# Two attention stages with transposes two units behind the scores, and new orders of work at the ends of three stages

## What is computed

```python
def swa_sink_attention(q, k, v, sinks):         # banded: 8 heads of 64, window 128
    ...
    sc = jnp.einsum('bnqkgd,bnjkd->bnkgqj', qb, kb).astype(jnp.float32) * (d ** -0.5)
    mask = (kpos <= qpos) & (qpos - kpos < w) & (kpos >= 0)
    sc = jnp.where(mask[None, :, None, None], sc, NEG_INF)
    p = jax.nn.softmax(jnp.concatenate([sc, sink], axis=-1), axis=-1)[..., :-1].astype(v.dtype)
    o = jnp.einsum('bnkgqj,bnjkd->bnqkgd', p, vb)

def forgetting_attention(q, k, v, fcum):        # 8 heads of 64, causal
    ...
        s = s + jnp.transpose(fq, (0, 2, 1))[..., None] - f_key[:, :, None, :]
        p = jax.nn.softmax(s, axis=-1).astype(v.dtype)

def even_mixer(h, ...):                         # before the latent attention:
    q = (rmsnorm(z_cq, q_norm) @ w_uq).reshape(b, s, MLA_HEADS, MLA_NOPE + MLA_ROPE)

def hgrn2_mixer(h, w_in, lb, gn_g, w_out):      # 8 heads, forward and backward scan
    ...
    o = o * lax.rsqrt(jnp.mean(o * o, axis=-1, keepdims=True) + EPS)
    o = o * gn_g.astype(jnp.float32).reshape(HGRN_HEADS, HGRN_DV)
    o = o.reshape(b_sz, s_len, D_MODEL).astype(h.dtype) * jax.nn.silu(g)
    return o @ w_out
```

## Time and profile before

| what | value |
|---|---|
| median of 3 runs | 2163.84 us (2163.27 to 2165.21) |
| the profiled execution | 2165.33 us, its span from the first to the last instruction 2163.5 us |
| PE busy | 2067.0 us, 96% of the span |
| DVE, ACT busy | 1459.0 us, 922.2 us |
| mean granted TensorE clock | 0.985 |

### The profile page before, as it was taken

One profiled execution on the slowest core, in us unless ns is written; L12 is line 12 of the kernel. 1 busy time (PEld: TensorE's weight loads), 2 busy tenths in 40 slices (PEclk: granted clock), 3 DMA queues, 4 the chain that ended last, 5 costly groups with the idle time before them and its releaser, 6 DMA issues.

```text
span 2163.5 us, 26466 instructions
## 1 busy us (share of the span) xinstructions
PE 2067.0 (96%) x9808; PEld 1589.4 (73%) x9808; DVE 1459.0 (67%) x2639; ACT 922.2 (43%) x1739; POOL 16.1 (1%) x15
## 2 busy tenths in 40 slices
PE   4989999999999999899999999999999899999998
PEld 2766566777667676578888887788888777888886
DVE  7667777666475799876555566989889865343343
ACT  3344554354443532343223235666666544232231
POOL 1000000000000000000000000000000000000000
PEclk8999999999999999999999999999999999999999
DMA  8522222533224111045555552111111122233221
GB/s 337 195 93 78 76 79 69 175 127 136 79 84 165 45 49 49 20 146 204 178 196 173 183 175 69 59 50 57 52 49 59 40 69 79 97 98 97 97 90 58
DMA packets 65982, 228.73 MB, mean 106 GB/s; under 512 B 7104, under 2 KB 9280, under 8 KB 65728
## 3 DMA queue, kind: packets, MB, share of 16 engines
q1 hardware_dynamic: 65856, 227.05, 30.9%
HBM read 224.93 MB, written 2.10 MB: 105 GB/s over the span
## 4 chain that ended last, share of the span: by engine, by line
PE 72%; DVE 17%; ACT 5%; issue 4%; DMA 1%; SPq 1%; DVEq 0%; ACTq 0%
PE bank L379 20%; PE bank L381 19%; PE bank L380 19%; DVE arena L1793 6%; PE bank L2079 3%; DVE w_lo L315 1%; PE bank L1242 1%; PE bank L688 1%; PE bank L1256 1%; PE bank L1267 1%; PE bank L987 1%; DMA arena<-ada_dram 1%; DVE arena L2025 1%; ACT w_hi L306 1%; ACT arena L1285 1%
## 5 line engine op out<-in xcount | busy, mean ns | idle before, releaser
L379 PE MATMUL bank<-h_hi,w_hi 128*128 128x512 f32 (+1 forms) x1564 | 643.1, 411 | 3.9 <-DVE h_lo L680 1.5
L381 PE MATMUL bank<-h_hi,w_lo 128*128 128x512 f32 (+1 forms) x1564 | 616.3, 394 | 0.0
L380 PE MATMUL bank<-h_lo,w_hi 128*128 128x512 f32 (+1 forms) x1564 | 614.5, 393 | 0.0
L306 ACT ACTIVATE w_hi<-w_raw 128x1024 fp32r<-128x1024 f32 (+3 forms) x293 | 290.7, 994 | 286.6 <-PE bank L381 273.6
L315 DVE TENSOR_TENSOR w_lo<-w_raw,w_hi 128x1024 fp32r<-128x1024 f32 (+3 forms) x290 | 333.3, 1151 | 73.9 <-ACT w_hi L306 73.5
L379 PEld LDWEIGHTS bank<-h_hi,w_hi 128*128 128x128 f32 (+1 forms) x1564 | 296.8, 190 | 71.9 <-issue 8.4
L381 PEld LDWEIGHTS bank<-h_hi,w_lo 128*128 128x128 f32 (+1 forms) x1564 | 295.6, 189 | 65.9
L380 PEld LDWEIGHTS bank<-h_lo,w_hi 128*128 128x128 f32 (+1 forms) x1564 | 296.8, 190 | 58.8 <-issue 3.8
L379 PE MATMUL bank<-a_hi_t,w_hi 128*128 128x512 f32 x512 | 203.0, 396 | 0.0
L380 PE MATMUL bank<-a_lo_t,w_hi 128*128 128x512 f32 x512 | 203.0, 396 | 0.0
L381 PE MATMUL bank<-a_hi_t,w_lo 128*128 128x512 f32 x512 | 203.0, 396 | 0.0
(11 more groups left out here) (276 smaller groups left out, 2496.2 us busy)
## 6 DMA issues: line engine op xcount, KB each, us to landing
w_raw<-weights_dram SPq DMA_DIRECT2D x261, 512.0 KB, 3.6
ada_raw<-ada_dram SPq DMA_DIRECT2D x128, 512.0 KB, 3.6
arena<-ada_dram SPq DMA_DIRECT2D x8, 1024.0 KB, 15.7
w_raw<-weights_dram SPq DMA_DIRECT2D x16, 256.0 KB, 2.5
xT<-x_dram SPq DMA_DIRECT2D x1, 2048.0 KB, 14.4
out_dram<-xT SPq DMA_DIRECT2D x8, 256.0 KB, 2.2
tables<-tables_dram SPq DMA_DIRECT2D x1, 1536.0 KB, 19.8
w_raw<-weights_dram SPq DMA_DIRECT2D x8, 144.0 KB, 3.5
```

The costliest lines, as they stand in the source:

```text
L306: nc.scalar.activation(WH[:, slot, 0:w], RAW[:, raw, 0:w], ACT.Copy).then_inc(w_hi_ready, 1)
L379: nc.tensor.matmul(o, WH[:, slot, cols], self.hi(k), start=(i == 0), stop=False)
L380: nc.tensor.matmul(o, WH[:, slot, cols], self.lo(k), start=False, stop=False)
L381: last = nc.tensor.matmul(o, WL[:, slot, cols], self.hi(k), start=False, stop=(i == self.K - 1))
```

## The change

1. `PairAttention` gets a parameter `lag`, 1 as before, and 2 in the banded and the forgetting attention. Transposes and PT copies of unit u-lag and sums of unit u-lag-1 stand with the scores of unit u. There are 2*lag+2 row buffers and columns of statistics, and the stage has two steps more.
2. In the banded attention's weave, `nq` writes its high part in place and its low part to free places, no longer over `HH` and `HL`. Its steps go from 26.7 to 14.7 and on, two apart; `pq` starts at 26.4 with 1.2 a tile, `nk` at 28.2.
3. In the forgetting attention's weave, the scratch of `hn` moves, and the seven blocks of `yp` go from 31.2 + 0.7i to 32.4 + 0.8i.
4. In head 7 of HGRN each slot splits one head's output, at the start of ACT's slot and not at its end; the blocks follow one slot later; a third tile's blocks go into the second direction's slots, and `HgrnEnd` gets a fourth tile's. The weight of the fourth tile is split ahead, in slots (1, 1) and (1, 2). Bank 6 serves as the fourth tile's bank. The norm behind it moves with it.

```diff
-                self.steps = 2 * U + 4
+                self.steps = 2 * U + 2 * lag + 2
...
-                if s % 2 == 0 and 2 <= u < U + 2:
-                    self.pe_sums(pe, u - 2)
-                if 1 <= u < U + 1:
-                    self.pe_turn(pe, u - 1, s % 2)
+                lag = self.lag
+                if s % 2 == 0 and lag + 1 <= u < U + lag + 1:
+                    self.pe_sums(pe, u - lag - 1)
+                if lag <= u < U + lag:
+                    self.pe_turn(pe, u - lag, s % 2)
...
-                if 1 <= u < U + 1:
-                    self.act_copy(act, u - 1, s % 2)
+                if self.lag <= u < U + self.lag:
+                    self.act_copy(act, u - self.lag, s % 2)
...
-                    if r >= 4:
-                        dve.wait_ge(self.turned.sem, self.turned.at(r - 3))
-                        dve.wait_ge(self.exp_ready.sem, self.exp_ready.at(r - 3))
+                    if r >= self.rows:
+                        dve.wait_ge(self.turned.sem, self.turned.at(r - self.rows + 1))
+                        dve.wait_ge(self.exp_ready.sem, self.exp_ready.at(r - self.rows + 1))
...
-            nq = Norm(Z[:, 0:3, :], 3, lambda k: vec("q_norm", k), None, HH, HL, 0, scratch=(view(16, (2, S)), view(20, (2, S)), None, view(28, (S,)), None),
+            NQ_HI = place_at("nq_hi", arena_offset + 48 * 1024, [P, 3, S], F32R)
+            NQ_LO = [place_at(f"nq_lo{k}", arena_offset + kb * 1024, [P, S], F32R) for k, kb in enumerate((44, 46, 76))]
+            nq_hi, nq_lo = lambda k: NQ_HI[:, k, :], lambda k: NQ_LO[k][:]
+            nq = Norm(Z[:, 0:3, :], 3, lambda k: vec("q_norm", k), None, nq_hi, nq_lo, 0, scratch=(view(16, (2, S)), view(20, (2, S)), None, view(28, (S,)), None),
...
-            weave((swa, 0, 1), (gates, 0.3, 0.8), (nq, 26.7, 0.3, 4, 8), (pq, 28.1, 0.9), (nk, 29.2, 1, 3, 6))
+            weave((swa, 0, 1), (gates, 0.3, 0.8), (nq, 14.7, 2, 4, 8), (pq, 26.4, 1.2), (nk, 28.2, 1, 3, 6))
...
-                  *((Do(lambda pe, i=i: yp.chunk(pe, i, range(3))), 31.2 + 0.7 * i, 1) for i in range(C - 1)))
+                  *((Do(lambda pe, i=i: yp.chunk(pe, i, range(3))), 32.4 + 0.8 * i, 1) for i in range(C - 1)))
...
-                    pr = Begun(8, C, P, HH, HL, [], residual(96 + 16), evac_engine="dve", chunks=H.split, outer=3)
-                    out = {"project": pr, (0, 1): ((0, 1), ()), (0, 2): ((2,), (0, 1)), (0, 3): ((3,), (2,)), (0, 4): ((4,), (3,)), (0, 5): ((5,), (4,)),
-                           (0, 6): ((), (5,)), (1, 0): ((6,), ()), (1, 1): ((), (6,))}
+                    pr = Begun(8, C, P, HH, HL, [], residual(96 + 16), evac_engine="dve", chunks=H.split, outer=4, banks=(0, 1, 2, 6), split_early=True)
+                    pr.before[3] = (H.applied.sem, H.applied.at(13))
+                    out = {"project": pr, (0, 1): ((0,), (), ()), (0, 2): ((1,), (0,), ()), (0, 3): ((2,), (1,), ()), (0, 4): ((3,), (2,), ()), (0, 5): ((4,), (3,), ()),
+                           (0, 6): ((5,), (4,), ()), (1, 0): ((6,), (5,), ()), (1, 1): ((), (6,), ()), (1, 2): ((), (), (0,)), (1, 3): ((), (), (1, 2)),
+                           (1, 4): ((), (), (3,)), (1, 5): ((), (), (4, 5)), (1, 6): ((), (), (6,))}
```

More of the change, by code:

```diff
@@ L443, in evacuate, with splits @@
                 self.evac(eng, bank[self.banks[t]], t, t % RING, t // 2, self.free)
+            def splits(self, t):
+                return t < self.count and self.n0 + t + AHEAD < N_TILES
             def act_step(self, act, i):
@@ L450, in act_tile @@
             def act_tile(self, act, t, p):
-                if t < self.count and p == 0 and self.n0 + t + AHEAD < N_TILES:
+                if self.splits(t) and p == 0:
                     split_hi(act, self.n0 + t + AHEAD)
@@ L467, in dve_tile @@
                     self.evacuate(dve, t)
-                if t < self.count and p == min(1, self.parts - 1) and self.n0 + t + AHEAD < N_TILES:
+                if self.splits(t) and p == min(1, self.parts - 1):
                     split_lo(dve, self.n0 + t + AHEAD)
@@ L499, in build, with __init__, early_hi, early_lo @@
         class Begun(Project):
+            def __init__(self, *args, split_early=False, **more):
+                Project.__init__(self, *args, **more)
+                self.split_early = split_early
+            def early_hi(self, act):
+                split_hi(act, self.n0 + AHEAD)
+            def early_lo(self, dve):
+                split_lo(dve, self.n0 + AHEAD)
+            def splits(self, t):
+                return Project.splits(self, t) and not (t == 0 and self.split_early)
             def chunk(self, pe, k, tiles=(0, 1)):
@@ L1187, in build, with __init__ @@
         class PairAttention(Stage):
-            def __init__(self, heads, scale, finish, e, pt, ready=(), window=False, sink=None, forget=None, made=None):
+            def __init__(self, heads, scale, finish, e, pt, ready=(), window=False, sink=None, forget=None, made=None, lag=1):
                 self.heads, self.scale, self.finish, self.E, self.PT = heads, scale, finish, e, pt
-                self.ready, self.window, self.sink, self.forget = ready, window, sink, forget
+                self.ready, self.window, self.sink, self.forget, self.lag, self.rows = ready, window, sink, forget, lag, 2 * lag + 2
                 self.made = made or {}
@@ L1210, in keys, with column @@
                 return range(i - 1 if self.window and i else 0, i + 1) if self.window else range(i + 1)
+            def column(self, which, r):
+                at = (8, 14, 20, 28)[which] + r % self.rows
+                return STAT[:, at:at + 1]
             def row_read(self, h):
@@ L1255, in pe_turn @@
                 for a in range(n):
-                    last = nc.tensor.transpose(bank[6][:, a * P:(a + 1) * P], self.E[r % 4][:, a * P:(a + 1) * P], ident)
+                    last = nc.tensor.transpose(bank[6][:, a * P:(a + 1) * P], self.E[r % self.rows][:, a * P:(a + 1) * P], ident)
                 last.then_inc(self.turned.sem, 1)
@@ L1307, in dve_step @@
                     return
-                done = u >= 2 and self.units[u - 2][1] == NT - 1
+                v = u - self.lag - 1
+                done = v >= 0 and self.units[v][1] == NT - 1
                 if done:
-                    g = self.units[u - 2][0]
-                    dve.wait_ge(self.out_done.sem, self.out_done.at(u - 1))
+                    g = self.units[v][0]
+                    dve.wait_ge(self.out_done.sem, self.out_done.at(v + 1))
                     self.finish.take(dve, g, self.out_read)
@@ L2223, in act @@
                 h, d = u // 2, u % 2
+                for k in self.out.get((d, l), ((), (), ()))[0]:
+                    H.high_act(act, k)
                 if l == 0:
@@ L2266, in act @@
                         H.key_act(act, u + 2)
-                for k in self.out.get((d, l), ((), ()))[0]:
-                    H.high_act(act, k)
+                    if not woven and l == 1:
+                        self.out["project"].early_hi(act)
             def dve(self, dve):
@@ L2321, in dve @@
                         H.times_sigmoid(dve, h, "g")
-                for k in self.out.get((d, l), ((), ()))[0]:
+                    if not woven and l == 2:
+                        self.out["project"].early_lo(dve)
+                for k in self.out.get((d, l), ((), (), ()))[0]:
                     H.low_dve(dve, k)
```

44 lines of the change are left out of this document (24 added, 20 removed).

## The result

The changed kernel takes 2170.29 us (median of 7 runs, 2168.32 to 2170.98) against 2163.84 in the same runs of the kernel before: ratio 1.0025, interval 1.0016 to 1.0035. It is slower by 0.25% where 0.5% faster was forecast. Its profiled execution had 2168.32 us, span 2166.5.

| stage, from which PE instruction to which | before | after | difference | forecast |
|---|---|---|---|---|
| banded: first score to the first score of the latent attention | 117.3 | 117.9 | +0.6 | -6.0 |
| forgetting: first score to the first sum of the norm behind `yp` | 151.2 | 158.9 | +7.7 | 0 |
| HGRN: last `pv_own` but one to the first sum of the norm behind `pr` | 80.3 | 74.8 | -5.4 | -4.9 |

The account below looks back on a forecast made before the run. PE was taken as the bound, busy 2067.0 of 2163.5 us, so only its idle or half-clock time could go. Banded -6.0, lag 0 and HGRN -4.9 sum to -10.9 us, from 2163.84 to 2153 (2149 to 2157), chance 0.50.

Parts of the forecast that it names:

- The lag in the forgetting attention: Forgetting attention: time saved at the first transpose is waited at the second, so 0 us, bounds -1.5 and +1.5.
- The banded stage: Banded attention: filling the idle hole at its end, less three costs, gives -6.0 us, bounds -8.1 and 0.
- I take all 8.1 us as removed: Banded attention's end: `pq` tiles cover 4.23 us of PE idle time and remove 3.9 lost at half clock.
- `nq` among the gate tiles: Banded attention, units 7 to 10: extra DVE scales and low parts delay maxima, +1.0 us, bounds 0 and 4.3.
- the last copy without cover: Banded attention's new end: last transpose, copy and sums have no tile between, so PE waits +0.6 us.
- the late `finish`: Banded attention's end: `finish` comes later against the next stage's rotary steps, +0.5 us, bounds 0 to 2.
- L1256 waits for L1297 outside that hole as before: Check for the banded attention: away from the filled hole, PE's transposes wait for ACT's copies as before.
- Lag in the banded stage: Banded attention: transposing two units behind the scores was to save nothing, 0 us.
- HGRN: HGRN's last head: earlier high parts and moved blocks fill PE's idle time, -4.9 us, bounds -10.6 and 0.
- C: Rival: the lag pays, removing remaining copy and weight waits and a half-clock stretch, -8.7 us, 2144; chance 0.14.
- D: Rival: the hole moves with `nq` and `pq`, the clock still falls, HGRN gives 1.5; 2162, no difference; chance 0.12.
- E: Rival: maxima come late at each of four `nq` places and the clock falls, +7 us, 2171; chance 0.06.

Follow-up runs that it names:

- x3: Changed kernel with only the banded attention back to lag 1, the forgetting one still at lag 2: 2168.95 us, ratio 1.0017 to the kernel before.
- x1: Changed kernel with both attentions back to lag 1 and the `yp` blocks at their old places: 2159.04 us, ratio 0.9975 to the kernel before.
- x2: Changed kernel with only the forgetting attention back to lag 1 and the old `yp` places: 2159.03 us, ratio 0.9978 to the kernel before.
- w2: Changed kernel, lag 2 kept, with the split behind the next unit's maxima and the last four `hn` parts later: 2160.52 us, ratio 0.9981.
- w1: Changed kernel with forgetting attention at lag 1, old `yp` places, and its split one unit later, where lag 2 puts it: 2162.55 us, ratio 0.9992.
- x4: Kernel before with only the new end of HGRN's last head: 2158.50 us, ratio 0.9967 to the kernel before.
- y4: Changed kernel with `nq`, `pq`, `nk` at old places, lag 2 in the banded attention and lag 1 in the forgetting one: 2163.64 us, ratio 0.9992.
- z4: Changed kernel with lag 1 in both attentions, old `yp` places, and the split behind the next unit's maxima: 2158.07 us, ratio 0.9977.
- z2: Changed kernel with lag 1 and old `yp` places in the forgetting attention, and the split behind the next unit's maxima: 2160.74 us, ratio 0.9973.
- y3: Changed kernel with forgetting attention at lag 1 and the modulation sums of `pq` behind its odd tiles: 2160.28 us, ratio 0.9977.

## Why the prediction was wrong

**The lag in the forgetting attention** (forecast 0, bounds -1.5 and +1.5; measured +7.7 in the stage, in the medians 9.9, `x3` against `x1`, to 11.3, after against `x2`). The step that failed is "I take 0 for the banded attention and 0 for the forgetting one", and in it the sum over one instruction pair. It followed transposes and copies, which the lag moves and which behave as said, and left out what else is tied to the older unit: the read of bank 7 and the split, 1.79 us of DVE, which moved a unit later and so ahead of the widest maximum. PE's queue, ACT's and DVE's were each walked for the transpose, DVE's not for `finish`. `finish` was named once, as a cost of 0.5 us at the stage's end. The runs showed in its place: +3.3 us idle and 11.1 us more at half clock (5.6 lost), less 1.1 that this sum does not explain (the idle time inside the slow stretches, 0.7 us, is counted one and a half times in it, which is 0.4). With the split moved behind the maxima the stage is 4.1 us shorter, with `hn` moved too 8.2 and as long as before; over both stages the two are worth 9.8 us of the changed kernel's time (`w2`). The split's place with lag 1 costs 1.4 us of idle time, and 3 to 3.5 us in time at the limit of what the runs can tell (`w1`). How much of the rest is the read of bank 7, which stands in front of PE's sums at once and can't be put off without delaying them, was not tried apart.

**The banded stage** (forecast -6.0, measured +0.6 in the profiles and nothing in the medians). "I take all 8.1 us as removed" is the step that failed. The hole and its slow stretch did go, and the clock gave more than forecast: 21.8 us at half level became 7.5, worth 7.2. But the idle time grew by 5.7 us. The largest waits are 2.97 for the read of bank 7 behind a weight's low part and a modulation tile, 2.52 for the maximum behind the split and `nk`, and 1.93 at 188.09 behind the split. Both figures lean on one execution of the kernel before: `x4`, with the same order of work there, had 11.4 us at half level and 13.2 idle. Nor is it the lag alone. `x1`, with the new order and lag 1, has 13.2 us idle too and a stage no shorter than `x4` (117.4 against 115.7): the 2.8 and the wait for `nq` are gone, and 1.3, 1.3 and 0.9 us stand at 209 to 213 in their place. Cover only helps if it stands ahead of the waiting instruction; the `pq` tiles stand between steps. The sizes for `nq` among the gate tiles (+1.0; 0.68 more idle, by `y4`), for the last copy without cover (+0.6; the sums waited 0.74 there) and for the late `finish` (+0.5; the rotary wait grew by 0.4) were of the right order. The check that I had named, "L1256 waits for L1297 outside that hole as before", came out wrong: 3.5 us (5.4 in `x4`) became 10.2.

**Lag in the banded stage** (forecast 0): 5 us with the old order of `nq` and `pq` (`y4` against `x4`), nothing with the new one (`x2` against `x1`).

**HGRN** (forecast -4.9, measured -5.4 in the trace, 5.8 in the medians of `x4`'s turns). The mechanism held: the waits for L2044 fell from 9.4 to 4.5 us, the one of 3.9 stayed at 3.8, and the fifth tile waits 0.39 us for its weight, where +0.4 was forecast and nothing stood before. The clock has no part in it: the stage has 3.4 us at half level in both kernels, and 11.6 us of idle time became 6.4. One sign came out otherwise: DVE still waits 1.96 us for the high part once (1728.87, against 4.13 before and the 1 us that the forecast asked for), at the cost of 0.38 us of PE. In all fifteen kernels with the new end this stage takes 74.1 to 74.9 us.

**Rivals.** C (the lag pays) did not occur: no pair of kernels that differ in the lag of one stage shows a gain in the medians. D came nearest for the banded stage: the hole moved. E had the right sum (2171) for the wrong reason: `nq` among the gate tiles added 0.68 us of waiting (`after` against `y4`) and there is no half-clock stretch between 165 and 185; the late maxima that cost most were two of the forgetting stage (627.79 and 656.24), behind the split. That ACT works its queue in order, which spoke against the lag, holds in the traces after ([6.78 <-DVE] and then the copies behind the exponential).

No version beats the simplest one by a margin that the runs can tell: `x4`, the kernel before with the HGRN end, at 2158.50 and 0.9967, is the simplest; the lowest median, 2158.07 and 0.9977, is `z4`'s. The parts in the two attentions can be left out.

## What to carry to other kernels

When a step is moved in hand-ordered queues, list everything that hangs on it, the work at the end of a group above all, and look at what it now stands in front of; 1.8 us ahead of the widest unit's maximum cost more than the 1.3 us wait that the move was to remove. Put work that nobody waits for behind the instruction on which the other engines wait: that one edit gave back 8.4 us of the changed kernel, though nothing that shows in the kernels with lag 1, where the work stood elsewhere. Before filling a hole, find the instruction that ends it, and ask whether the filler stands ahead of it in the waiting engine's queue.

## What the runs showed of the chip

The length of the forgetting stage is 141.7 us plus PE's idle time plus half of the time at half clock, in all kernels with lag 1 within 0.4 us, and 0.2 to 1.2 less with lag 2. Idle time inside the slow stretches explains at most 0.5 of that (0.7 us of it in the changed kernel, 0.9 in `x3`, 0.1 or none in the others); the rest stays open. The two terms make up the difference between 148.5 us (`x2`) and 158.9 to about 1.3 us. The Trainium skill ("TensorE: Matmul & The Clock Gate", section "Terms") prices the throttled time in just this way; as a sum over a stage with idle time beside it the traces agree with it to about 1 us.

A slow stretch can also hide waiting. `before` and `x4` have the same order of work in the banded stage and 21.8 against 11.4 us at half level, which would be 5.2 us of time; but they have 10.6 against 13.2 us idle, and the stages differ by 1.6. Within a slow stretch of `before` the transpose at 161.39 us waited 0.36 us, at full clock in `x4` the same one 1.61.

What I had not expected is how loosely the slow stretches go with the idle time. `x2` and `z2` have the same 4.8 and 4.9 us idle in the forgetting stage and 3.3 against 12.6 us at half clock. The executions of one kernel differ in the same way: of the eleven of `z2` five lie at 2154.2 to 2156.3 us and six at 2160.7 to 2162.3, and none between. Two slow stretches of the changed kernel stand right behind waits of 1.8 and 2.2 us, but six kernels with lag 1 have one between 624 and 637 us as well; in `y3` (629.9 to 636.7) it stands behind waits of 1.34 and 0.69 us, and `x2` has the same two waits and no slow stretch. A gain of 4 us in one stage of one profile can be lost by such a stretch later; what decides in which executions it falls, no run here shows.
